# Retention of a streaming encoder: scores of diagonal blocks and running state sums in place of all causal blocks

## The chip, the cores and the metric

The kernel runs on one core of one Trainium2 chip. The time is that of one launch on the device, in microseconds (us). TensorE is the matrix engine (PE in the rows; PEld is its weight load, the load of the stationary operand), VectorE is DVE, ScalarE is ACT, GpSimd is POOL, and SyncE (SP) only issues transfers. The time before is 2163.48 us, the median of three runs (2162.94 to 2163.66).

## What is computed

Two layers of an encoder, for 512 new tokens of one stream (the prompt) and 32 tokens of a running stream (the sample). A layer is a mixer (a retention branch of 4 heads and an attention branch of 8 heads, merged by gates) and a gated feed-forward. Only the retention changes. In the reference it goes by chunks of 64 tokens, with a state S per head (128 x 256):

```python
scores = einsum('bihd,bjhd->bhij', q, k) * decay            # decay[i,j] = g^(i-j) for i >= j, else 0
o = einsum('bhij,bjhe->bihe', scores, v) + einsum('bihd,bhde->bihe', q, S) * xi
S_new = S * g_len + einsum('bjhd,bjhe->bhde', k * zeta, v)
```

Here g is a number per head just below 1, q and k have 128 columns per head and v has 256. Behind it o is normed per head and token, multiplied by a gate silu(g_r), and projected. The last S is an output. The result does not depend on the length of a chunk, so a kernel may choose another.

## The kernel before, in words

All products that need fp32 precision are made of three matmuls: each operand is split into a high part, rounded to the fp32r type, and a low part, which is the operand less its high part; the three are high x high, high x low and low x high. ScalarE makes the high part (a copy that rounds), VectorE the low part (a subtraction that writes fp32r). For the weights GpSimd does the subtraction.

Each engine has its own program, written out in the order in which it runs: `sync_program`, `pool_program`, `pe_program`, `act_program`, `dve_program`. They meet only at semaphores. `S.up(name, key)` counts one up, and `S.at(name, key)` is the wait for it. `S.own()` is the wait for the engine's own last result. A bank of PSUM is taken by `acquire(bank, act=, dve=)` on TensorE, which waits until ScalarE and VectorE have counted up `act_free_<bank>` and `dve_free_<bank>` for the bank's last user. There are eight banks: mm0 and mm1, used in turn by the projections, s0, s0b, s1, s1b, t and o.

A layer has six phases: S, D (four times, attention), R (retention), M (merge), F and G (feed-forward). The weights come in units of 2048 columns per partition, which are split in two halves of 1024: ScalarE's `hi` (L1157) makes the high half, GpSimd's `lo` (L519) subtracts it from the raw one. ScalarE starts the pair of the next unit ahead of tile 0 of the unit at hand.

Phase R runs over the four heads, and there are two layers, so that the head's part is run 8 times. Per head there are three units of weights: query and key (`rk`), value (`vr`) and gate (`gr`). A unit is multiplied by `n_tile(j, m)` in five tiles of tokens: tile 4 is the 32 samples (fp32 matmuls, L682), and tiles 0 to 3 are 24 matmuls of 256 columns each (L703 to L705). The retention itself stands between the tiles of the gate's unit. TensorE's order for a head, from line 913:

- tiles of the value's unit, then 10 transposes of rotated queries and keys (L726, from `rk`) to banks s0 and s1, as soon as VectorE's rotation is done (key `rope`, L1976 to L1988)
- `n_tile(j, 4)`, `n_tile(j, 0)`, `rscores(0)`, `rscores(1)`, `n_tile(j, 1)`, `rscores(2)`, `rscores(3)`, `n_tile(j, 2)`, `outs(0)`, `outs(1)`, the sample's scores (L981), `n_tile(j, 3)`, `outs(2)`, `outs(3)`, the new state (12 matmuls, L991), the sample's output (L997, L998) and the sample's new state (L1002)

`rscores(jb)` (L936) multiplies the keys of block jb with the queries of blocks jb to 3: 512, 384, 256 and 128 columns, three matmuls each. `outs(ib)` (L950) adds up, for the queries of block ib, the products of the weighted scores with the values of blocks 0 to ib, three matmuls of 256 columns for each pair of blocks.

VectorE's order for a head (L1976 to L2095): the rotation; the low parts of the value's tiles (`value_lo`, L1969), which free the banks mm0 and mm1; the keys times zeta (L1992, key `kz`); the sample's sum (L1760, L1764); `qx` (L1999); the low parts of the transposed queries and keys (L2003); the sample's gate sum (L2045, L2048, key `gsum`), which frees the bank of `n_tile(j, 4)`, the one that `n_tile(j, 1)` takes; then `gate(0)` to `gate(3)` (L2011) with the scores times decay (`decayed`, L2028), their low parts (`decayed_lo`, L2018), and `gated(ib)` (L2038), which multiplies an output block in bank t or o by its gate. ScalarE's `squares(hh, ib)` (L1655) reads the same bank, and both must be through before the bank is taken again. The low part of the keys times zeta (L2069, `kz_lo`) comes late, behind `gated(1)`.

Of the kernel before, what the change touches and what calls it, by code (L numbers as in the profile page):

```python
# [43 lines left out]
F32 = mybir.dt.float32  # L44
F32R = mybir.dt.float32r
# [37 lines left out]
def shape_tables():  # L83
# [16 lines left out]
    rel = np.arange(SEQ, dtype=f)[None, :] - np.arange(P, dtype=f)[:, None]  # L100
    decay = np.where(rel[:, None, :] >= 0, np.exp(log_g[None, :, None] * np.maximum(rel, 0)[:, None, :]), 0) * ks
    zeta = np.zeros((P, TILES, RET_HEADS), f)
    for m in range(NT):
        zeta[:, m] = np.exp(log_g * (SEQ - 1.0 - pos[:, m:m + 1])) * ks
    zeta[:DEC, NT] = np.exp(log_g * (DEC - 1.0 - np.arange(DEC, dtype=f)[:, None])) * ks
    xi = np.exp(log_g[:, None] * (np.arange(DEC, dtype=f) + 1.0))
# [3 lines left out]
        zeta.reshape(P, -1), np.broadcast_to(xi.reshape(1, -1), (P, RET_HEADS * DEC)),  # L110
        np.broadcast_to(np.exp(log_g * f(DEC))[None], (P, RET_HEADS)),
        np.broadcast_to(np.array([[lam[0], lam[1], 1 - lam[0], 1 - lam[1]]]), (P, 4))], axis=1)
    return small.astype(f), np.ascontiguousarray(decay.astype(f).reshape(P, RET_HEADS * SEQ))
# [110 lines left out]
def program(nc, A, known):  # L224
# [4 lines left out]
    with ctx:  # L229
# [29 lines left out]
        nsmall = P + 2 * TILES * 64 + 2 * TILES * 8 + TILES * 4 + 4 * DEC + 4 + 4  # L259
# [13 lines left out]
        zeta = take(TILES * 4).rearrange("p (m h) -> p m h", m=TILES)  # L273
        xi = take(4 * DEC).rearrange("p (h i) -> p h i", h=4)
# [29 lines left out]
        sT_hi = sb("sT_hi", [P, NT * UC], F32R, base)  # L304
        rk_sample = sb("rk_sample", [P, UC], F32, base)
# [18 lines left out]
        with ExitStack() as s:  # L324
            with ExitStack() as s2:
                sT_raw = sb("sT_raw", [P, 1280], F32, s2)
                kz_raw = sb("kz_raw", [P, TILES, RET_DK], F32, s2)
            sT = sb("sT", [P, 1280], F32R, s)
            kz = sb("kz", [P, TILES, RET_DK], F32R, s)
            vrh = sb("vrh", [P, 2, NT, UC], F32R, s)  # L330
            sT_hi2 = sb("sT_hi2", [P, 2 * P], F32R, s)
# [3 lines left out]
            decay = sb("decay", [P, SEQ], F32, s)  # L335
            oret = sb("oret", [P, KC, TILES, P], F32, s)
# [80 lines left out]
        def sync_program(S):  # L417
# [28 lines left out]
            for l in S.layers():  # L446
                for phase, _ in ORDER:
                    for i in S.bodies(phase):
# [25 lines left out]
                        elif phase == "R":  # L474
                            for j, what in enumerate(us):
# [10 lines left out]
                                if j % 3 == 1 and j < 11:  # L486
                                    h = j // 3
                                    e.wait_ge(*(S.at("dve_free_s1", ("snew", h - 1)) if h else S.at("dve_free_s1", k=0)))
                                    e.dma_start(decay[:, :], A["tab_decay"][:, h * SEQ:(h + 1) * SEQ]).then_inc(*S.up("decay_in", ("d", h), n=16))
# [110 lines left out]
        def pe_program(S):  # L600
# [134 lines left out]
            for _ in S.layers():  # L735
# [180 lines left out]
                for _ in S.bodies("R"):  # L916
                    start()
                    tile[0] = 0
                    for hh in range(RET_HEADS):
# [16 lines left out]
                        def rscores(jb):  # L936
                            n = SEQ - jb * P
                            if jb == 0:
                                e.wait_ge(*S.at("act_free_s1", ("qk", hh, 1)))
                                e.wait_ge(*S.at("dve_free_s1", ("qk", hh, 1)))  # L940
                                acquire("s0", dve=2)
                            if jb == 2:
                                acquire("s1", dve=2)
                            bank = "s0" if jb < 2 else "s1"
                            for i, (a, b) in enumerate(((0, 0), (1, 0), (0, 1))):
                                ins = e.matmul(pv(bank, P, n, (jb % 2) * 512), key_part(b)[:, jb * P:(jb + 1) * P], qrT[:, a, jb * P:SEQ],
                                               start=(i == 0), stop=(i == 2))
                            ins.then_inc(*S.up("s_ready", ("ret", hh, jb)))

                        def outs(ib):  # L950
                            bank = "to"[ib % 2]
                            acquire(bank, act=1, dve=1)
                            e.wait_ge(*S.at("dve_step", ("sT_lo", hh, ib)))
                            if hh == 0 and ib == 1:
                                e.wait_ge(*S.at("osum_done", "osum"))
                            if ib == 0:
                                e.wait_ge(*S.at("dve_free_mm0", ("vr", hh, 2)))
                                e.wait_ge(*S.at("dve_free_mm1", ("vr", hh, 3)))
                            for jb in range(ib + 1):
                                o = SOFF[jb] + (ib - jb) * P  # L960
                                hi = sT_hi_part(jb)[:, (ib - jb) * P:(ib - jb + 1) * P]
                                for i, (s, v) in enumerate(((hi, 0), (hi, 1), (sT[:, o:o + P], 0))):
                                    ins = e.matmul(pv(bank, P, RET_DV), s, vrh[:, v, jb, :],  # L963
                                                   start=(jb == 0 and i == 0), stop=(jb == ib and i == 2))
# [5 lines left out]
                        rscores(0)  # L970
                        rscores(1)
# [1445 lines left out]
```

## Time and profile before

| | |
|---|---|
| median of three runs | 2163.48 us |
| the profiled execution's own time | 2163.2 us |
| its span in the trace | 2161.4 us |
| TensorE matmul busy | 2142.2 us, 17696 matmuls |
| VectorE, ScalarE, GpSimd busy | 1207.6, 974.3, 871.0 us |
| granted TensorE clock | 1.00 |
| one head of phase R | 47.25 us, 8 times |

Busy time of TensorE counts every moment at which a matmul is in flight. Matmuls overlap, so the duration of one (283 ns for 256 columns) is not what it costs: that is read from the start of one to the start of the next. A row of a timeline with x2 merges two instructions, and its first number is the start of the first.

### The profile page before, as it was taken

Reading aid. Unit: us, or ns where it says so; the run is one execution under the profiler, and the core shown is the slowest. Engines: PE = TensorE matmul, PEld = TensorE weight load, DVE = VectorE, ACT = ScalarE, POOL = GpSimd, SP = SyncE. Lnnn points to the kernel's source line nnn. Section 1 sums busy time; section 2 is a strip of 40 time slices with the busy share of each in tenths; the row PEclk is TensorE's granted clock in tenths of the full one; section 3 lists DMA queues with packets and bytes.
Section 4 is the critical chain, followed back from the end, with each engine's and each line's share of the span. In section 5 each row is a group of like instructions: output and inputs, shape, how many; then the busy total and the mean of one; then the engine's idle time right before and its main releaser. Section 6 shows DMA issues by size and latency. Waiting matters only on the chain.

```text
span 2161.4 us, 43436 instructions
## 1 busy us (share of the span) xinstructions
PE 2142.2 (99%) x17696; PEld 2080.4 (96%) x17696; DVE 1207.6 (56%) x2107; ACT 974.3 (45%) x1882; POOL 871.0 (40%) x386
## 2 busy tenths in 40 slices
PE   7999999999999999999999999999999999999999
PEld 7899989999999999999998899999999999999999
DVE  6676666556355662266267576655563556623551
ACT  5655564445323452344246655644542335423441
POOL 4344423234433433433463354323343444334433
PEclk9999999999999999999999999999999999999999
DMA  5323222222222222221323233222222222222223
GB/s 176 100 85 114 74 84 86 72 96 79 79 88 89 82 83 82 98 98 61 107 92 101 75 105 100 72 72 89 79 82 95 79 86 92 80 88 98 90 69 109
DMA packets 76405, 193.71 MB, mean 90 GB/s; under 512 B 7760, under 2 KB 28848, under 8 KB 76208
## 3 DMA queue, kind: packets, MB, share of 16 engines
q1 hardware_dynamic: 67712, 184.51, 25.9%
q10 hardware_dynamic: 8496, 6.44, 0.9%
q8 instruction: 141, 2.31, 0.4%
q14 instruction: 56, 0.46, 0.1%
HBM read 177.50 MB, written 13.42 MB: 88 GB/s over the span
## 4 chain that ended last, share of the span: by engine, by line
PE 89%; DVE 7%; ACT 3%; issue 1%; DMA 0%; DVEq 0%; ACTq 0%
PE ps L654 13%; PE ps L656 13%; PE ps L655 13%; PE ps L703 7%; PE ps L704 7%; PE ps L705 7%; PE ps L1093 4%; PE ps L1092 4%; PE ps L1094 4%; DVE nmax L1895 2%; PE ps L682 2%; PE ps L726 2%; PE ps L800 1%; PE ps L802 1%; PE ps L801 1%; PE ps L963 1%
## 5 line engine op out<-in xcount | busy, mean ns | idle before, releaser
L519 POOL TENSOR_TENSOR wlo<-raw,whi 128x1024 fp32r<-128x1024 f32 (+1 forms) x328 | 769.8, 2367 | 1043.0 <-ACT whi L1157 1043.0
L654 PE MATMUL ps<-hl,whi 128*128 128x272 f32 x2432 | 703.0, 289 | 0.0
L656 PE MATMUL ps<-hl,wlo 128*128 128x272 f32 x2432 | 701.0, 288 | 0.0
L655 PE MATMUL ps<-hl,whi 128*128 128x272 f32 x2432 | 699.8, 288 | 0.0
L654 PEld LDWEIGHTS ps<-hl,whi 128*128 128x128 f32 x2432 | 458.7, 189 | 0.0
L656 PEld LDWEIGHTS ps<-hl,wlo 128*128 128x128 f32 x2432 | 457.5, 188 | 0.0
L655 PEld LDWEIGHTS ps<-hl,whi 128*128 128x128 f32 x2432 | 457.1, 188 | 0.0
L1157 ACT ACTIVATE whi<-raw 128x1024 fp32r<-128x1024 f32 (+1 forms) x330 | 314.2, 997 | 204.1 <-PE ps L1094 179.4
L703 PE MATMUL ps<-whi,hl 128*128 128x256 f32 x1216 | 347.0, 285 | 0.0
L704 PE MATMUL ps<-wlo,hl 128*128 128x256 f32 x1216 | 343.0, 282 | 0.0
L705 PE MATMUL ps<-whi,hl 128*128 128x256 f32 x1216 | 342.6, 282 | 0.0
L703 PEld LDWEIGHTS ps<-whi,hl 128*128 128x128 f32 x1216 | 230.1, 189 | 10.7 <-issue 10.7
L705 PEld LDWEIGHTS ps<-whi,hl 128*128 128x128 f32 x1216 | 230.0, 189 | 0.0
L704 PEld LDWEIGHTS ps<-wlo,hl 128*128 128x128 f32 x1216 | 229.4, 189 | 0.0
L1093 PE MATMUL ps<-act,whi 128*128 128x272 f32 (+1 forms) x704 | 203.8, 290 | 0.0
L1092 PE MATMUL ps<-act,whi 128*128 128x272 f32 (+1 forms) x704 | 203.1, 289 | 0.0
L1094 PE MATMUL ps<-act,wlo 128*128 128x272 f32 (+1 forms) x704 | 202.8, 288 | 0.0
L2234 DVE SCALAR_TENSOR_TENSOR ca<-up,par,ca 128x546 f32<-128x546 f32 x176 | 141.6, 804 | 37.2 <-ACT ca L1568 29.5
L1092 PEld LDWEIGHTS ps<-act,whi 128*128 128x128 f32 x704 | 132.9, 189 | 0.3
L1094 PEld LDWEIGHTS ps<-act,wlo 128*128 128x128 f32 x704 | 133.0, 189 | 0.0
L1093 PEld LDWEIGHTS ps<-act,whi 128*128 128x128 f32 x704 | 132.8, 189 | 0.0
L525 POOL TENSOR_TENSOR rstd<-ms,mhalf 128x20 f32<-128x20 f32 x20 | 79.5, 3973 | 109.8 <-DVE ms L1672 108.9
(241 smaller groups left out, 3314.9 us busy)
## 6 DMA issues: line engine op xcount, KB each, us to landing
raw<-in_w_units_dram SPq DMA_DIRECT2D x260, 512.0 KB, 4.7
raw<-in_w_down_units_dram SPq DMA_DIRECT2D x64, 352.0 KB, 3.5
kcT<-in_cache_k_dram SPq DMA_DIRECT2D x16, 256.0 KB, 2.9
out_new_k_prompt_dram<-rawk SPq DMA_DIRECT2D x8, 512.0 KB, 3.0
out_new_v_prompt_dram<-vd SPq DMA_DIRECT2D x8, 512.0 KB, 3.6
raw<-in_w_first_dram SPq DMA_DIRECT2D x6, 512.0 KB, 4.9
vc_n<-in_cache_v_dram SPq DMA_DIRECT2D x8, 256.0 KB, 4.5
vc_n<-in_cache_v_dram ACTq DMA_DIRECT2D x8, 256.0 KB, 2.8
```

Of the source, the lines that this page charges most:

```text
L519: e.tensor_tensor(wlo[:, s, a:b], raw[:, s, a:b], whi[:, s, a:b].bitcast(F32), ALU.subtract).then_inc(*S.up("w_ready", ("lo", j, part)))
L654: e.matmul(out, wh, hi, start=(c == 0), stop=False)
L655: e.matmul(out, wh, lo, start=False, stop=False)
L656: ins = e.matmul(out, wl, hi, start=False, stop=(c == KC - 1))
L703: e.matmul(out, hi, wh, start=(c == 0), stop=False)
L704: e.matmul(out, hi, wl, start=False, stop=False)
L705: ins = e.matmul(out, lo, wh, start=False, stop=(c == KC - 1))
L1092: e.matmul(out, wh, hi, start=(k == 0), stop=False)
L1093: e.matmul(out, wh, lo, start=False, stop=False)
L1094: ins = e.matmul(out, wl, hi, start=False, stop=(k == FB - 1))
L1157: e.activation(whi[:, s, a:b], raw[:, s, a:b], ACT.Copy).then_inc(*S.up("hi_ready", ("hi", j, part)))
L2234: e.scalar_tensor_tensor(out=ca[:, s, :], in0=up[:, j % 2, s, v:v + GP], scalar=w(2 + v, j, s), in1=ca[:, s, :], op0=ALU.mult, op1=ALU.add ...
```

## The change

Queries and keys are scaled ahead of the transposes: the query of token t by g^(t-511), its key by g^(511-t) (the table `zeta` has both now). Their product then has the decay g^(i-j) by itself, and the scores need only a mask of zeros and ones (`causal`), the same for every head. So scores are formed for the four diagonal blocks alone (`block_scores`). The blocks on their left are reached through sums: `state(m)` is the product of the scaled keys and the values of block m, `part_sum(m)` adds it to a running sum, and `outs(ib)` multiplies the query block with the sum of the blocks before it (`past`). The last sum is the new state, so that the 12 matmuls of L991 are the same ones, in four pieces. The table of decays and its transfers go.

```diff
-        sT_hi = sb("sT_hi", [P, NT * UC], F32R, base)
+        sb("rk_space", [P, TILES, UC], F32, base)
...
+            zq = sb("zq", [P, TILES, 2, RET_DK], F32, s)
+            sT_raw = sb("sT_raw", [P, NT, P], F32, s)
+            sT = sb("sT", [P, 2, NT, P], F32R, s)
+            kz = sb("kz", [P, NT, RET_DK], F32R, s)
+            past = sb("past", [P, 2, NT - 1, RET_DV], F32R, s)
+            state_sum = sb("state_sum", [P, RET_DV], F32, s)
...
-                                    e.dma_start(decay[:, :], A["tab_decay"][:, h * SEQ:(h + 1) * SEQ])...
```

TensorE:

```diff
-                        e.wait_ge(*S.at("dve_step", ("rope", hh)))
+                        e.wait_ge(*S.at("dve_step", ("zq", hh)))
                         for v in range(2):
-                            feature_transposes(lambda m: rk[:, m, v * P:(v + 1) * P], f"s{v}", ("qk", hh, v), 1, 1)
+                            feature_transposes(lambda m: zq[:, m, v, :], f"s{v}", ("qk", hh, v), 1, 1)
...
+                        def block_scores():
+                            e.wait_ge(*S.at("act_free_s1", ("qk", hh, 1)))
+                            e.wait_ge(*S.at("dve_free_s1", ("qk", hh, 1)))
+                            acquire("s0", dve=2)
+                            for b in range(NT):
+                                tokens = slice(b * P, (b + 1) * P)
+                                for i, (q, k) in enumerate(((0, 0), (1, 0), (0, 1))):
+                                    ins = e.matmul(pv("s0", P, P, b * P), key_part(k)[:, tokens], qrT[:, q, tokens], start=(i == 0), stop=(i == 2))
+                            ins.then_inc(*S.up("s_ready", ("ret", hh)))
+                            for i, (q, k) in enumerate(((0, 0), (1, 0), (0, 1))):
+                                ins = e.matmul(pv("s0b", P, DEC), key_part(k)[:, SEQ:SEQ + P], qrT[:, q, SEQ:TOK], start=(i == 0), stop=(i == 2))
+                            ins.then_inc(*S.up("s_ready", ("rets", hh)))
+                        def state(m):
+                            bank = PART_BANKS[m % 2]
+                            acquire(bank, dve=1)
+                            if m == 0:
+                                e.wait_ge(*S.at("dve_free_mm0", ("vr", hh, 2)))
+                                e.wait_ge(*S.at("dve_free_mm1", ("vr", hh, 3)))
+                                e.wait_ge(*S.at("dve_step", ("kz_lo", hh)))
+                            for i, (z, v) in enumerate(((kzh, 0), (kzh, 1), (kz, 0))):
+                                ins = e.matmul(pv(bank, P, RET_DV), z[:, m, :], vrh[:, v, m, :], start=(i == 0), stop=(i == 2))
...
                         def outs(ib):
-                            for jb in range(ib + 1):
-                                o = SOFF[jb] + (ib - jb) * P
-                                hi = sT_hi_part(jb)[:, (ib - jb) * P:(ib - jb + 1) * P]
-                                for i, (s, v) in enumerate(((hi, 0), (hi, 1), (sT[:, o:o + P], 0))):
+                            for i, (a, v) in enumerate(((0, 0), (0, 1), (1, 0))):
+                                ins = e.matmul(pv(bank, P, RET_DV), sT[:, a, ib, :], vrh[:, v, ib, :], start=(i == 0), stop=(ib == 0 and i == 2))
+                            if ib:
+                                e.wait_ge(*S.at("dve_step", ("past_lo", hh, ib - 1)))
+                                for i, (a, v) in enumerate(((0, 0), (0, 1), (1, 0))):
+                                    ins = e.matmul(pv(bank, P, RET_DV), qrT[:, a, ib * P:(ib + 1) * P], past[:, v, ib - 1, :], start=False, stop=(i == 2))
...
-                        rscores(0)
-                        rscores(1)
+                        block_scores()
+                        state(0)
                         n_tile(j, 1, hl1, dve=1, act=1)
-                        rscores(2)
-                        rscores(3)
+                        state(1)
+                        outs(0)
                         n_tile(j, 2, hl1, dve=1, act=1)
-                        outs(0)
+                        state(2)
                         outs(1)
...
                         n_tile(j, 3, hl1, dve=1, act=1)
+                        state(3)
                         outs(2)
                         outs(3)
...
+                        acquire("s0", dve=1)
+                        e.matmul(pv("s0", P, RET_DV), zq[:, NT, 1, :], rk[:, NT, :], start=True, stop=True)...
                         acquire("t", act=1, dve=1)
```

VectorE and ScalarE:

```diff
+                        e.tensor_tensor(zq[:, :, :, :], rk[:, :, :].rearrange("p m (v d) -> p m v d", v=2),
+                                        zeta[:, :, :, head:head + 1].broadcast_to([P, TILES, 2, P]), ALU.mult)...
                         value_lo(2)
-                        e.tensor_tensor(kz_raw[:, :, :], rk[:, :, P:2 * P], zeta[...], ALU.mult)...
                         value_lo(3)
...
+                        e.wait_ge(*S.at("act_step", ("kzh", hh)))
+                        e.wait_ge(*S.own())
+                        e.tensor_tensor(kz[:, :, :], zq[:, 0:NT, 1, :], kzh[:, :, :].bitcast(F32), ALU.subtract)...
...
                         gate(0)
-                        decayed(0)
-                        decayed(1)
-                        decayed_lo(0)
-                        decayed_lo(1)
+                        masked()
+                        part_sum(0)
+                        masked_lo()
+                        part_lo(0)
                         gate(1)
...
                         gate(3)
+                        part_sum(3)
                         gated(2)
                         gated(3)
...
                                 if u == 2 and m in (2, 3):
-                                    for ib in ((0, 1) if m == 2 else (2, 3)):
-                                        squares(S, e, hh, ib)
+                                    squares(S, e, hh, m - 2)
...
+                        squares(S, e, hh, 2)
+                        squares(S, e, hh, 3)
                         squares(S, e, hh, NT)
```

`masked` is the scores times the mask, for the four blocks and for the sample; `masked_lo` their low part (a subtraction of 512 columns, SBUF to SBUF); `part_lo(m)` the low part of a running sum. ScalarE copies the high parts behind the tanh of gate tiles 0, 1 and 2. SyncE loses its transfer of the decays.

VectorE's order in the second head of a layer, from the end of the rotation to the first gate, before (`kz_raw` are the keys times zeta, `vrh` the value's tiles, `rest` the sample's sums):

```order
L1988 TENSOR_TENSOR rawq<-rawq,kz_raw 128x10x64
L1969 SCALAR_TENSOR_TENSOR vrh<-ps,rs,vrh 128x256
L1992 TENSOR_TENSOR kz_raw<-rawq,small 128x640
L1969 SCALAR_TENSOR_TENSOR vrh<-ps,rs,vrh 128x256
L1760 SCALAR_TENSOR_TENSOR rest<-ps,rs,rest 32x256 x2
L1764 SCALAR_TENSOR_TENSOR rawq<-ps,rs,rest 32x256
L1999 TENSOR_TENSOR qx<-ps,small 128x32
L2003 TENSOR_TENSOR qrT<-ps,qrT 128x544
L2003 TENSOR_TENSOR krT_lo<-ps,krT 128x640
L2045 TENSOR_TENSOR rest<-ps,rest 32x256 x2
L2048 TENSOR_TENSOR rest<-ps,rest 32x256
L2011 SCALAR_TENSOR_TENSOR oret<-oret,ps 128x2x128
```

and the same stretch of the changed kernel:

```order
L1974 TENSOR_TENSOR rawq<-rawq,zq 128x10x64
L1977 TENSOR_TENSOR zq<-rawq,small 128x1280
L1955 SCALAR_TENSOR_TENSOR vrh<-ps,rs,vrh 128x256 x2
L1746 SCALAR_TENSOR_TENSOR rest<-ps,rs,rest 32x256 x2
L1750 SCALAR_TENSOR_TENSOR rawq<-ps,rs,rest 32x256
L1986 TENSOR_SCALAR qx<-ps,small 128x32
L1990 TENSOR_TENSOR qrT<-ps,qrT 128x544
L1990 TENSOR_TENSOR krT_lo<-ps,krT 128x640
L1994 TENSOR_TENSOR kz<-zq,kzh 128x512
L2057 TENSOR_TENSOR rest<-ps,rest 32x256 x2
L2060 TENSOR_TENSOR rest<-ps,rest 32x256
L2002 SCALAR_TENSOR_TENSOR oret<-oret,ps 128x2x128
```

The scaling has grown from 640 to 1280 columns and stands ahead of the value's low parts, where the transposes wait for it; the low part of the scaled keys now stands ahead of the sample's sums.

TensorE's order in the same head of the changed kernel, from the last two blocks of scores to the first matmul of gate tile 1 (`kzh` and `kz` are the parts of the scaled keys):

```order
L941 MATMUL ps<-qrT,krT 128x128 x2
L941 MATMUL ps<-qrT,krT_lo 128x128
L944 MATMUL ps<-qrT,krT 128x32 x2
L944 MATMUL ps<-qrT,krT_lo 128x32
L956 MATMUL ps<-vrh,kzh 128x256 x2
L956 MATMUL ps<-vrh,kz 128x256
L700 MATMUL ps<-whi,hl 128x256
```

Before, six matmuls of L946 (512 and 384 columns) stood ahead of that tile, and the three of 32 columns (L981) two tiles later.

## Rows read from the trace of the kernel before

**Rows 1.** The page's first part: busy time and share of the span.
```profile
PE 2142.2 (99%) x17696; PEld 2080.4 (96%) x17696; DVE 1207.6 (56%) x2107; ACT 974.3 (45%) x1882; POOL 871.0 (40%) x386
```
**Rows 2.** Waits of PE, whole span: us in total, times, longest us.
```profile
PE ps L746 <- DVE wlo L1709: 12.0, 1, 12.0
```
**Rows 3.** Timeline of PE, first head: start us, us, engine, line, operation.
```profile
324.53 0.62 PE L946 MATMUL ps<-qrT,krT 128*128 128x512 f32 x2
...
325.74 0.28 PE L703 MATMUL ps<-whi,hl 128*128 128x256 f32 x1
...
328.95 0.33 PE L946 MATMUL ps<-qrT,krT 128*128 128x128 f32 x2
...
329.23 0.33 PE L703 MATMUL ps<-whi,hl 128*128 128x256 f32 x1
329.40 0.28 PE L704 MATMUL ps<-wlo,hl 128*128 128x256 f32 x1
...
332.14 0.40 PE L963 MATMUL ps<-vrh,sT_hi 128*128 128x256 f32 x2
...
332.49 0.40 PE L963 MATMUL ps<-vrh,sT_hi 128*128 128x256 f32 x2
```
**Rows 4.** Timeline of DVE, second head, from the rotation to the scores' low parts.
```profile
360.30 1.16 DVE L1983 TENSOR_TENSOR rawq<-rawq,small 128x640 f32<-128x640 f32 x1
...
364.44 0.83 DVE L1988 TENSOR_TENSOR rawq<-rawq,kz_raw 128x640 f32<-128x640 f32 x1
...
370.27 0.81 DVE L2003 TENSOR_TENSOR krT_lo<-ps,krT 128x640 fp32r<-128x640 f32 x1
371.19 0.88 DVE L2045 TENSOR_TENSOR rest<-ps,rest 32x256 f32<-32x256 f32 x2
372.10 0.41 DVE L2048 TENSOR_TENSOR rest<-ps,rest 32x256 f32<-32x256 f32 x1
...
374.63 2.37 DVE L2018 TENSOR_TENSOR sT<-sT_raw,sT_hi 128x512 fp32r<-128x512 f32 x2
```
**Rows 5.** Timeline of POOL, second head.
```profile
358.38 5.34 POOL L519 TENSOR_TENSOR wlo<-raw,whi 128x1024 fp32r<-128x1024 f32 x2 [7.07 <-ACT whi L1157]
371.02 4.77 POOL L519 TENSOR_TENSOR wlo<-raw,whi 128x1024 fp32r<-128x1024 f32 x2 [7.30 <-ACT whi L1157]
```
**Rows 6.** Instructions of line 2069, eight heads: duration ns min/median/max.
```profile
L2069 DVE TENSOR_TENSOR kz<-kz_raw,kzh x8: 692/693/694, 334.7 to 1548.7; 128x512 fp32r<-128x512 f32 x8
```
**Rows 7.** Timeline of PE, second head: the first scores.
```profile
371.75 0.62 PE L946 MATMUL ps<-qrT,krT 128*128 128x512 f32 x2
```
**Rows 8.** Timeline of PEld (weight loads), second head.
```profile
366.49 1.12 PEld L726 LDWEIGHTS ps<-small,rawq 128*128 128x128 f32 x10
...
383.53 0.31 PEld L963 LDWEIGHTS ps<-vrh,sT_hi 128*128 128x128 f32 x2
...
387.83 0.40 PEld L998 LDWEIGHTS ps<-sq,qx 128*128 128x128 f32 x2
388.26 0.41 PEld L1002 LDWEIGHTS ps<-rawq,kz_raw 128*128 128x128 f32 x2
```
**Rows 9.** Timeline of DVE, then ACT, second head: outs(2) is gated and squared.
```profile
384.92 0.42 DVE L2038 TENSOR_TENSOR oret<-ps,oret 128x256 f32<-128x256 f32 x1
...
385.38 0.39 ACT L1662 ACTIVATE sq<-ps 128x256 f32<-128x256 f32 x1 [1.06 <-DVE oret L2038]
385.66 0.20 ACT L1662 ACTIVATION_READ_ACCUMULATOR sq<-ps 128x1 f32 x1
```
**Rows 10.** Timelines of DVE and PEld in phase D: a result, and who waits.
```profile
136.54 0.35 DVE L1917 SCALAR_TENSOR_TENSOR prob<-prob,rinv 128x128 f32<-128x128 f32 x1
...
137.10 0.14 PEld L857 LDWEIGHTS ps<-small,prob 128*128 128x128 f32 x1
```
**Rows 11.** Timelines of DVE and PEld, first head: rotation's end, transposes.
```profile
316.81 0.82 DVE L1988 TENSOR_TENSOR rawq<-rawq,kz_raw 128x640 f32<-128x640 f32 x1
...
319.27 1.12 PEld L726 LDWEIGHTS ps<-small,rawq 128*128 128x128 f32 x10
```

More of the change, by code:

```diff
@@ L999, in pe_program @@
                             *S.up("t_ready", ("os", hh)))
-                        acquire("s1", dve=1)
-                        e.matmul(pv("s1", P, RET_DV), kz_raw[:, NT, :], rk[:, NT, :], start=True, stop=True).then_inc(
-                            *S.up("s_ready", ("snew", hh)))
                 for _ in S.bodies("M"):
@@ L1998, in dve_program @@
                         e.wait_ge(*S.own())
-                        e.tensor_tensor(qx[:, 0:DEC], pv("s0", P, DEC, SEQ), xi[:, head, :], ALU.mult).then_inc(
+                        e.tensor_scalar(qx[:, 0:DEC], pv("s0", P, DEC, SEQ), g32[:, head:head + 1], None, ALU.mult).then_inc(
                             *S.up("dve_step", key=("qx0", hh)))
@@ new lines, in masked, with masked_lo @@
+                            e.wait_ge(*S.at("s_ready", ("rets", hh)))
+                            e.wait_ge(*S.own())
+                            e.tensor_tensor(sTs_x[0:DEC, 0:DEC], pv("s0b", DEC, DEC), causal[0:DEC, 0:DEC], ALU.mult).then_inc(
+                                *S.up("dve_free_s0", ("sTs", hh)))
+                        def masked_lo():
+                            e.wait_ge(*S.at("act_step", ("sT", hh)))
+                            e.wait_ge(*S.own())
+                            e.tensor_tensor(sT[:, 1, :, :], sT_raw[:, :, :], sT[:, 0, :, :].bitcast(F32), ALU.subtract).then_inc(
+                                *S.up("dve_step", key=("sT_lo", hh)))
@@ new lines, in part_sum @@
+                        def part_sum(m):
+                            bank = PART_BANKS[m % 2]
+                            e.wait_ge(*S.at("s_ready", ("part", hh, m)))
+                            if m == NT - 1:
+                                e.wait_ge(*(S.at("st_out0", ("st", hh - 1)) if hh else S.at("st_out0", k=0)))
+                            e.wait_ge(*S.own())
+                            if m == 0:
+                                ins = e.tensor_copy(state_sum[:, :], pv(bank, P, RET_DV))
+                            else:
+                                ins = e.tensor_tensor(sout[:, 0, :] if m == NT - 1 else state_sum[:, :], pv(bank, P, RET_DV), state_sum[:, :], ALU.add)
+                            ins.then_inc(*S.up(f"dve_free_{bank}", ("part", hh, m)))
@@ L2031, in gated, with part_lo @@
+                        def part_lo(m):
+                            e.wait_ge(*S.at("act_step", ("past", hh, m)))
+                            e.wait_ge(*S.own())
+                            e.tensor_tensor(past[:, 1, m, :], state_sum[:, :], past[:, 0, m, :].bitcast(F32), ALU.subtract).then_inc(
+                                *S.up("dve_step", key=("past_lo", hh, m)))
                         def gated(ib):
```

153 lines of the change are left out of this document (47 added, 106 removed).

## The prediction, made before the changed kernel was run

> **What bounds the kernel now.** I read the page's busy times first: a matmul is in flight for 99% of the span [rows 1]. Then the waits of TensorE: the longest entry is a single one of 12.0 us while the first weights are made ready [rows 2], and none of its entries lies in the retention. So TensorE's instruction stream is the time, and in phase R it has no holes. Whatever is taken out of it is gained in full, and whatever makes it wait is lost in full. Every other engine matters only where it hands something to TensorE, so the second reading is of margins: the timelines of VectorE, GpSimd and ScalarE in one head. The head runs 8 times, and its pattern repeats to within 0.2 us.
>
> **What TensorE loses in work.** Costs are distances from start to start. `rscores(0)` and `rscores(1)` take 324.53 to 325.74 = 1.21 us. The last three matmuls of 128 columns take 328.95 to 329.23 = 0.28, and the matmul behind them comes 0.17 after the next instead of the usual 0.12, so 0.33 in all: 0.11 for each [rows 3]. Three of 256 columns take 0.35 (332.14 to 332.49) [rows 3], 0.12 each. The old scores so cost 1.21 + 0.35 + 0.33 = 1.89 us per head. The new ones are 12 matmuls of 128 columns at 0.11 = 1.32: half the columns and more are gone, but a narrow matmul costs nearly what one of 256 does, because each brings a weight load of its own. Saved: 0.57. The outputs go from 30 matmuls to 21 (12 on the diagonal, 9 with the sums), 9 x 0.12 = 1.08 saved. The state's 12, the sample's matmuls and the transposes stay in number. Together **1.65 us saved per head**, 13.2 in all. The Trainium skill, "TensorE: Matmul & The Clock Gate", section "Wait — 56ns, not 53.3ns?", gives N / 2.4 GHz + about 2.5 ns from start to start, 56 ns for 128 columns. By that rule the new scores would be 0.67 and the old ones 1.63, and the forecast some 2.5 us lower; the rows' 0.11 speaks against it here, where every matmul loads new weights, and the sum goes by the rows.
>
> **First wait: the transposes.** They waited for the end of the rotation, and now wait for a multiplication of 1280 columns behind it. No row has that size. 256 columns take 0.41 and 640 take 0.83 [rows 4], which is 0.42 for 384 more; the next 640 add 0.70, and 1280 take 1.5. The bounds are 0.83 (its half) and 1.66 (twice that). From a result of VectorE to the weight load that waits for it go 0.21 us (136.54 + 0.35 to 137.10) [rows 10]. In the second head the rotation ends at 364.44 + 0.83 = 365.27 [rows 4]; the multiplication then ends at about 366.8, and the weight load may start at 367.0. It started at 366.49 [rows 8]. So 0.5 us of wait (0 to 0.7). In the first head of a layer it is 316.81 + 0.82 = 317.63, plus 1.5 and 0.21, 319.35, against 319.27 [rows 11]: 0.1. `value_lo(2)` and `value_lo(3)` are moved behind it, but their banks are wanted only after 10 transposes, which is more than their 0.48 each: nothing. The separate multiplication of 640 columns that goes is not on the path.
>
> **Second wait: the low part of the scaled keys**, and this one decides. It moves ahead of the sample's gate sum. It is a subtraction of 512 columns from SBUF to SBUF that took 0.69 us in all eight heads, late in the head with GpSimd idle [rows 6]. Where GpSimd's subtraction of weights runs, the like do not take that. In the trace of before, two low parts of scores (512 and 384 columns) issued at 374.63 took 2.37 where 0.69 + 0.56 would do [rows 4]: the extra 1.1 us is what GpSimd had left of its pair, which ends at 371.02 + 4.77 = 375.79 [rows 5]. The rotation's product at 360.30 took 1.16 instead of 0.83: it got in when the first half ended (358.38 + 2.39 = 360.77), and GpSimd's pair grew from 4.77 to 5.34 [rows 4, 5]. So each instruction holds the other out for its whole length, and VectorE gets in between two halves. Instructions that read a bank of PSUM are not held: the sample's gate sum at 371.19 ran its 0.88 right under GpSimd's [rows 4, 5]. The moved subtraction takes just the place of that sum: issued at 371.19, while GpSimd has begun at 371.02. It waits to 371.02 + 2.39 = 373.41 and ends at 374.10. The gate sum follows 0.11 later (the gap from `krT_lo` to it, 371.08 to 371.19) and takes 372.10 + 0.41 - 371.19 = 1.32 [rows 4], to 375.53. TensorE wants that bank for `n_tile(j, 1)`: 371.75 [rows 7] plus 15 narrow matmuls at 0.11 and the three of `state(0)` at 0.12 gives 373.76. It gets it at 375.53 + 0.21, and the first matmul comes 0.12 later, 375.86. **2.1 us of wait**. `state(0)` waits for the same subtraction, inside the same hole. The bounds are 0 (the subtraction goes first: gate sum at 373.2 + 0.21, in time) and 4.5 (it waits for both halves).
>
> Behind it all else is shifted alike. The masked scores (0.69 like the other 512 columns), ScalarE's copy, the copy of the sum and `masked_lo` (0.69) need about 2.9 us from the gate sum on, and TensorE has a tile of 24 matmuls and `state(1)`, 3.2 us; GpSimd's second half, pushed to 374.1, is over at 376.5, before `masked_lo` is issued. Nothing, then, though the cover is thin. `past_lo(0)` to `past_lo(2)` have most of a tile each.
>
> **Third wait: the end of the head.** The state's four products stood between `outs(3)` and the sample's output, which takes bank t again; three of them now lie before the last tile, and one ahead of `outs(2)`. TensorE's first weight load behind tile 3 is at 383.53; 15 matmuls at 0.12 (`state(3)`, two outputs of six) and the sample's state (387.83 to 388.26, 0.43) bring it to 385.76 [rows 8]. Bank t is free when `gated(2)` and its square are done. `gated(2)` ran at 384.92; `part_sum(3)` goes ahead of it now (0.42 and a gap of 0.11), so 385.45 to 385.87; the square and the read of its sum end 0.48 after they start (385.38 to 385.86) [rows 9], 386.39, and TensorE hears of it at most 0.2 later: 386.5. **0.7 us of wait** (0.3 to 1.0). Part of it falls at bank o, whose `squares(1)` is now behind the tanh of tile 3.
>
> ScalarE has fewer columns to copy, and SyncE one transfer fewer per head; the wait for `snew` ahead of SyncE's load of the state is the same event under another bank's name. None is on the path.
>
> **The sum.** Six heads: -1.65 + 0.5 + 2.1 + 0.7 = +1.65, 9.9 us. Two first heads: -1.65 + 0.1 + 2.1 + 0.7 = +1.25, 2.5 us. The profiled execution took 2163.2 us, so 2175.6; the median of the runs lies 0.3 above it, **2175.9 us**, slower by 0.6%. Its own range, by the bounds of the three waits, is 2169 to 2182.
>
> **The rivals.**
> *VectorE gets in first.* The two requests are 0.17 us apart [rows 4, 5]; if `qx`, now another form of instruction, or a copy of ScalarE's shifts that, the subtraction ends at 371.9, GpSimd's pair runs to 376.7, and the gate sum is in time. But then `masked_lo`, issued near 375.5, is held to 376.7, ends at 377.4, and `outs(0)` waits some 0.7. With the other waits a head comes to +0.25 (first heads -0.15): about 2165. For it: the distance is small. Against it: GpSimd was ahead in all eight heads. Chance 0.14.
> *Faster: neither subtraction is held.* If VectorE and GpSimd work side by side on these operands, the second wait is gone and a head comes to -0.45 (first heads -0.85): 2159. If the multiplication of 1280 columns and the end of the head fit in their margins too, it is the whole 13.2 us, 2150. The point is whether the gate sum ends before 373.4. Against it: rows of the same form, stretched in every head. Chance 0.13.
> *Held through both halves.* If GpSimd's second half goes first, 2.4 us more per head, 2195. The rotation's product got in between, eight times. Chance 0.05.
> *The scores are not cheaper.* If a narrow matmul into a bank shared by four blocks costs twice the 0.11, 1.3 us more per head, 2186; three in a row show nothing of it. Chance 0.03.
> The rest, 0.65, is the forecast.
>
> **How the numbers follow.** A measurement of this kernel tells about 0.2% from no change, 4.3 us: faster is below 2159.2, slower above 2167.8. Slower: the forecast less a little at its lower edge, the third and the fourth rival, 0.70. Same: the first rival and a share of the second's 2159, 0.17. Faster: 0.13. The range reaches from 2159, to take in the first rival and the edge of the second, to 2182, the upper end of the forecast's own; about 2 in 10 is left out.
>
> **What would show it.** Right: in every head the new low part of the keys with 2.5 to 3 us instead of 0.69, GpSimd's pair grown by 0.7 just there, a hole of about 2 us ahead of the first matmul of gate tile 1, smaller ones at the transposes and ahead of the sample's output, and 72 fewer matmuls. Wrong: the subtraction at 0.69 with GpSimd's first half starting behind it, narrow scores apart by other than 0.11, or a head shorter than the old one.

## The result, and the profile after

The changed kernel takes 2180.32 us (median of 5 runs, 2179.89 to 2181.86) against 2162.94 us for the one before (5 runs, 2162.16 to 2163.66): 17.4 us slower, a ratio of 1.0081 with a 95% interval of 1.0068 to 1.0094. The forecast was 2175.9 in a range of 2159 to 2182, and slower with a chance of 0.70. The direction and the mechanism held, and the time lies in the range, near its upper end; the loss of 17.4 us is 5 us more than the 12.4 that the sum gave.

The changed kernel's page, first the span and the busy times [rows 1]:

```profile
span 2178.5 us, 43278 instructions
PE 2142.9 (98%) x17624; PEld 2073.0 (95%) x17624; DVE 1230.4 (56%) x2115; ACT 970.1 (45%) x1874; POOL 872.1 (40%) x386
```

There are 72 matmuls fewer, and the span is 17.1 us longer. TensorE has less to do and takes longer over it: it waits. Its waits are where one reads on [rows 2]. This is the view of waits of the changed kernel, for PE (us in total, times, longest us) and then for PEld, where a wait shows as the idle time ahead of a weight load:

```profile
PE ps L743 <- DVE wlo L1695: 11.9, 1, 11.9
PE ps L700 <- DVE rest L2060: 7.1, 8, 1.2
PE ps L956 <- DVE kz L1994: 4.6, 8, 0.6
PE ps L672 <- DVE sq L2090: 2.7, 2, 1.3
```
```profile
PEld ps L700 <- issue: 19.4, 35, 1.4
PEld ps L956 <- issue: 5.1, 8, 0.7
PEld ps L996 <- ACT sq L1648: 3.8, 8, 0.5
PEld ps L672 <- issue: 3.4, 2, 1.7
PEld ps L967 <- ACT sq L1648: 2.1, 8, 0.3
PEld ps L723 <- DVE zq L1977: 2.0, 7, 0.3
```

Each of the eight heads now has a wait for the low part of the scaled keys (L956) and one for the gate sum's bank (L700), the two halves of one hole; two at the end of the head, at bank o (L967) and at bank t (L996); seven have one at the transposes (L723). L672 was in no list of mine: it is a fourth wait, twice, at the start of phase M.

The hole, in the second head. First VectorE, then GpSimd, then the weight loads of TensorE, three timelines [rows 4, 5, 8]:

```profile
371.17 0.81 DVE L1990 TENSOR_TENSOR krT_lo<-ps,krT 128x640 fp32r<-128x640 f32 x1
372.09 2.69 DVE L1994 TENSOR_TENSOR kz<-zq,kzh 128x512 fp32r<-128x512 f32 x1
374.89 0.88 DVE L2057 TENSOR_TENSOR rest<-ps,rest 32x256 f32<-32x256 f32 x2
375.80 0.41 DVE L2060 TENSOR_TENSOR rest<-ps,rest 32x256 f32<-32x256 f32 x1
```
```profile
371.86 5.15 POOL L516 TENSOR_TENSOR wlo<-raw,whi 128x1024 fp32r<-128x1024 f32 x2 [7.57 <-ACT whi L1148]
```
```profile
374.06 0.19 PEld L944 LDWEIGHTS ps<-qrT,krT_lo 128*128 128x128 f32 x1
374.90 0.30 PEld L956 LDWEIGHTS ps<-vrh,kzh 128*128 128x128 f32 x2 [0.65 <-issue]
375.13 0.19 PEld L956 LDWEIGHTS ps<-vrh,kz 128*128 128x128 f32 x1
376.33 0.19 PEld L700 LDWEIGHTS ps<-whi,hl 128*128 128x128 f32 x1 [1.01 <-issue]
```

The subtraction of 512 columns was issued at 372.09, 0.23 us behind GpSimd's start, and took 2.69 us in place of 0.69 [rows 6]. The gate sum, which reads PSUM, ran at its usual 0.88 and 0.41, but from 374.89 on. TensorE's weight loads stood for 0.65 and then for 1.01 us.

One more thing is in this trace. Its windows, two heads of the first layer and two of the second, then 4 us of the second head (us; busy us and instructions of PE, PEld, DVE, ACT, POOL; granted clock; DMA):

```profile
367.40:417.20 49.80, 48.19 (x400) 45.07 (x400) 30.25 (x48) 21.49 (x45) 16.37 (x7) 0.97 0.23 73
417.20:465.50 48.30, 46.67 (x400) 43.55 (x400) 30.30 (x48) 21.51 (x45) 16.38 (x7) 1.00 0.23 74
1399.10:1448.80 49.70, 48.15 (x400) 45.03 (x400) 30.17 (x48) 21.44 (x45) 16.36 (x7) 0.97 0.22 73
1448.80:1497.10 48.30, 46.67 (x400) 43.54 (x400) 30.30 (x48) 21.52 (x45) 16.38 (x7) 1.00 0.23 75
```
```profile
376.00:378.00 2.00, 1.64 (x11) 1.67 (x12) 1.58 (x5) 0.43 (x1) 1.00 (x1) 0.79 0.00 0
378.00:380.00 2.00, 2.00 (x11) 2.00 (x11) 1.47 (x3) 0.62 (x2) 0.00 (x0) 0.50 0.00 0
380.00:382.00 2.00, 2.00 (x17) 2.00 (x17) 0.42 (x1) 0.47 (x1) 0.00 (x0) 0.86 0.00 0
```

The heads have two lengths, 48.3 and 49.8 us, where before all had 47.2. The 400 matmuls are the same. In the longer ones the granted clock falls to 0.50, the 1.2 GHz level, for 3.4 us behind the hole (TensorE had stood for most of 374.3 to 376.3), and 11 matmuls pass in 2 us instead of 19. That happened in three of the eight heads of this execution, 1.5 us each, 4.5 us together. Not every hole does this. The fourth wait leaves one of 1.7 us at the start of phase M in each layer, and there the clock stays at 1.00:

```profile
490.09 0.52 PEld L672 LDWEIGHTS ps<-small,rs 128*128 128x128 f32 x5 [1.71 <-issue]
```
```profile
488.00:494.00 6.00, 4.67 (x36) 4.27 (x35) 2.21 (x7) 3.02 (x10) 1.17 (x1) 1.00 0.14 46
```

The first row is that hole in the first layer, the second the stretch around it. By the Trainium skill, "TensorE: Matmul & The Clock Gate", section "What's actually happening", the throttled state is the default and activity releases it; the trace agrees in so far as each of the three falls stands behind a hole; which holes bring one these rows do not tell.

**Where the 17.1 us come from.** The rows of idle weight loads name the waits: transposes 2.0, hole 5.1 + 8.7 (L700's 19.4 less the 10.7 that it had before the change), end of the head 3.8 + 2.1, phase M 3.4. For a sum they are too short. A weight load lasts 0.19 us, but in a stream without waits the next one begins 0.11 or 0.12 after it, so that a wait costs some 0.07 more than the idle time in its row. In the second head 2.27 us pass from the load at 374.06 to the one at 376.33, where without waits it would be 0.11 + 3 x 0.12 = 0.47: 1.80 us lost, and the rows show 0.65 + 1.01.

Distances have no such gap. From the first transpose of one head to that of the next it is 47.22 us before and 48.29 now, if the clock stays at 1.00: 1.07 more, net of the work saved. Six such distances make 6.4 us, and three falls of the clock 4.5. The other 6.2 us lie behind the last head of each layer (2.6 and 3.1, with phase M's wait of 1.7 in each) and ahead of the second layer's first head (0.65), less 0.17 at the start.

### The profile page after: what moved, and what is told of

Its sections match the earlier page's. It is cut to its first block, busy times and chain, and to the rows that moved or that the text cites. A ratio compares the mean times of both kernels' runs of the same rounds, so it can differ in the third digit from the quotient of the medians.

```text
span 2178.5 us, 43278 instructions
## 1 busy us (share of the span) xinstructions
PE 2142.9 (98%) x17624; PEld 2073.0 (95%) x17624; DVE 1230.4 (56%) x2115; ACT 970.1 (45%) x1874; POOL 872.1 (40%) x386
## 4 chain that ended last, share of the span: by engine, by line
PE 82%; DVE 12%; ACT 3%; issue 1%; DMA 0%; DVEq 0%; POOL 0%; ACTq 0%
PE ps L651 13%; PE ps L653 13%; PE ps L652 13%; PE ps L700 6%; PE ps L701 6%; PE ps L702 6%; PE ps L1088 4%; PE ps L1087 4%; PE ps L1089 4%; DVE nmax L1881 2%; PE ps L723 2%; PE ps L797 1%; PE ps L799 1%; PE ps L798 1%; PE ps L679 1%
## 5 line engine op out<-in xcount | busy, mean ns | idle before, releaser
L700 PE MATMUL ps<-whi,hl 128*128 128x256 f32 x1216 | 348.9, 287 | 7.6 <-DVE rest L2060 7.1
L700 PEld LDWEIGHTS ps<-whi,hl 128*128 128x128 f32 x1216 | 232.3, 191 | 20.3 <-issue 19.4
```

The costliest lines, as they stand in the source:

```text
L700: e.matmul(out, hi, wh, start=(c == 0), stop=False)
```

## The experiments

Two theories of the hole. *Theory 1*: GpSimd's weight subtraction holds VectorE's out for its whole length. *Theory 2*: the subtraction is slow by itself, by its operands or by its place behind ScalarE's copy, or nothing is held and only the queue got longer. The first four runs test these and the fourth wait.

**GpSimd waits for the low part of the keys.** In the changed kernel's GpSimd program:

```diff
                     for j in range(1, UNITS["R"] + 1):
+                        if j % 3 == 2:
+                            e.wait_ge(*S.at("dve_step", ("kz_lo", j // 3)))
                         lo("R", j)
```

> The changed kernel, but GpSimd waits with its weight subtraction for the low part of the scaled keys, so that VectorE's subtraction is never issued into a running one of GpSimd. Theory 1 (GpSimd holds it out): it takes 0.69 us instead of 2.69, the hole ahead of gate tile 1 (about 2 us per head) is gone, and with it the three stretches of 3.4 us at a granted clock of 0.50; but masked_lo is now issued into GpSimd's second half, takes some 1.9 us, and outs(0) waits about 0.7 us per head. 2180.3 - 8 x 2.1 - 4.5 + 8 x 0.75 = 2165. Theory 2 (the subtraction is slow by its own operands or its place behind ScalarE's copy, and GpSimd is beside the point): it stays at 2.7 us, and so does the hole: 2180, or more by what the weights come late.

Measured: 2165.66 us (11 runs, 2165.01 to 2166.66), 1.0014 of before (1.0005 to 1.0022). VectorE and GpSimd of this run, second head:

```profile
370.42 0.69 DVE L1996 TENSOR_TENSOR kz<-zq,kzh 128x512 fp32r<-128x512 f32 x1
371.21 0.88 DVE L2059 TENSOR_TENSOR rest<-ps,rest 32x256 f32<-32x256 f32 x2
...
374.78 1.70 DVE L2022 TENSOR_TENSOR sT<-sT_raw,sT 128x512 fp32r<-128x512 f32 x1
```
```profile
371.19 4.75 POOL L516 TENSOR_TENSOR wlo<-raw,whi 128x1024 fp32r<-128x1024 f32 x2 [8.57 <-DVE kz L1996]
```

The same instruction with the same operands in the same place takes 0.69 us once GpSimd is not running. Theory 2 is out. The cost has gone to the next subtraction from SBUF to SBUF: `masked_lo` took 1.70, and `outs(0)` waited for it (weight loads of L969 idle 3.6 us in eight heads, against none). That is the mechanism of my first rival, only that it had to be forced. Its price, 2165, fits by some luck: this run has the 3.4 us of phase M, which the rival's sum had not, and a wait at `outs(0)` below the 0.7 us per head that it had. The clock stayed at 1.00 throughout.

**Gate sum first.** On VectorE alone:

```diff
-                        e.tensor_tensor(kz[:, :, :], zq[:, 0:NT, 1, :], kzh[:, :, :].bitcast(F32), ALU.subtract)...
...
                             *S.up(f"dve_free_{bank}", ("gsum", hh)))
+                        e.tensor_tensor(kz[:, :, :], zq[:, 0:NT, 1, :], kzh[:, :, :].bitcast(F32), ALU.subtract)...
                         gate(0)
```

> The changed kernel, with the low part of the scaled keys moved behind the sample's gate sum on VectorE; TensorE's order stays. Theory 1: it is issued at 1.4 us later into the same GpSimd instruction and ends at the same moment, 2.7 us after GpSimd's start, so state(0) waits as before (0.6 to 0.7 us per head), but the bank of gate tile 1 is free in time: the hole shrinks from 2.0 to about 0.7 us, no stretch at clock 0.50: 2180.3 - 8 x 1.3 - 4.5 = 2165. Theory 2: the subtraction takes 2.7 us from its later start, state(0) waits 1.4 us longer than now and the hole keeps its length: 2180.

Measured: 2167.11 us (11 runs, 2166.6 to 2167.93), 1.0021 (1.0012 to 1.003). Its VectorE and GpSimd, second head:

```profile
370.70 0.88 DVE L2053 TENSOR_TENSOR rest<-ps,rest 32x256 f32<-32x256 f32 x2
371.62 0.41 DVE L2056 TENSOR_TENSOR rest<-ps,rest 32x256 f32<-32x256 f32 x1
372.13 1.27 DVE L2060 TENSOR_TENSOR kz<-zq,kzh 128x512 fp32r<-128x512 f32 x1
```
```profile
370.48 5.18 POOL L516 TENSOR_TENSOR wlo<-raw,whi 128x1024 fp32r<-128x1024 f32 x2 [7.57 <-ACT whi L1148]
```

Issued 1.6 us behind GpSimd's start it took 1.27, issued 0.23 behind it 2.69: in both cases it ends 2.9 us after that start (2.92 in each). So its duration says only how much of GpSimd's half was left. `state(0)` waits as before (5.1 us in eight heads), the bank is free in time (L700 back to 11.0 us), and the clock does not fall, behind these eight short holes or behind phase M's two of 1.7 and 1.8 us. One line in another place gained 13.2 us.

**And `state(0)` behind gate tile 1**, with its sum behind `gate(1)` and ScalarE's copy of that sum behind the tanh of tile 1 in place of tile 0 (not shown):

```diff
                         block_scores()
-                        state(0)
                         n_tile(j, 1, hl1, dve=1, act=1)
+                        state(0)
                         state(1)
...
                         masked()
-                        part_sum(0)
                         masked_lo()
-                        part_lo(0)
                         gate(1)
+                        part_sum(0)
+                        part_lo(0)
                         part_sum(1)
```

> As the run before, and state(0) moved behind gate tile 1 on TensorE, with its sum behind gate(1) on VectorE. Theory 1: no hole at all ahead of gate tile 1: 2180.3 - 8 x 2.1 - 4.5 = 2159, below the kernel before by some 4 us. If the clock did not fall because of that hole, the stretches at 0.50 stay and it is 2163.5. Theory 2: the subtraction is still 2.7 us, hidden behind the tile; gate(0) comes late, the masked scores with it, and outs(0) waits: 2163 to 2168.

Measured: 2161.51 us (11 runs, 2161.02 to 2162.14), 0.9995 (0.9986 to 1.0004): no difference from before that can be measured. The wait of L956 is gone from the list and nothing stands in its place. It is 2.5 us above what was expected, as the run before was 2.1 above: the hole was 1.80 us per head and not the 2.1 I had put down, 8 x 0.3 us.

**The spread of phase M in other banks.**

```diff
-                    spread("s0", "s0b")
+                    spread("s1", "s1b")
```

> The changed kernel, with the first transposes of phase M (the spread of the norms) in banks s1 and s1b instead of s0 and s0b. The theory of a fourth wait (bank s0 is held by the last head's new state of the sample until VectorE has read it, behind the sample's output): the wait of 1.7 us at the start of phase M goes in both layers: 2180.3 - 3.4 = 2176.9. Its rival (the spread waits for the norms' own values, whichever bank it takes): 2180.3.

Measured: 2175.28 us (5 runs, 2174.97 to 2177.68), 1.0061 (1.0049 to 1.0074): 5.0 us less. The waits of L672 (2.7 us of PE, 3.4 of PEld) are out of its list, the waits of the heads are to the tenth those of the changed kernel. Most of the other 1.6 us is a fall of the clock less, two heads instead of three in its profile. The rival, that the spread waits for the norms' own values, is out. So the bank is the cause: the change gave the sample's new state to s0, VectorE reads it last of all in a head, and the next phase begins with s0.

The other four runs: the same suspicion in the kernel before, the remaining waits, and all of them at once.

**One line of the change in the kernel before**: its low part of the keys (L2069) moved ahead of its gate sum, nothing else.

```diff
+                        e.tensor_tensor(kz[:, 0:NT, :], kz_raw[:, 0:NT, :], kzh[:, :, :].bitcast(F32), ALU.subtract)...
...
                         gated(1)
...
-                        e.tensor_tensor(kz[:, 0:NT, :], kz_raw[:, 0:NT, :], kzh[:, :, :].bitcast(F32), ALU.subtract)...
                         gate(3)
```

> The kernel before, with one thing of the change alone: the low part of the scaled keys moved ahead of the sample's gate sum on VectorE. Theory 1 (held by GpSimd's weight subtraction): it takes 2.7 us there, the gate sum ends near 375.6 instead of 372.5 in the second head, and gate tile 1 waits some 2.9 us per head: 8 x 2.9 = 23 us, and a hole this long should bring TensorE's clock to 0.50 for 3.4 us in some or all heads, 1.5 us each: 2162.7 + 23 + 0 to 13 = 2186 to 2199. Theory 2 (no hold, only 0.69 us more in the queue, of which 0.1 is margin): 8 x 0.6 = 5 us, 2167.5, and no fall of the clock.

Measured: 2196.03 us (4 runs, 2194.07 to 2196.91), 1.0153 (1.014 to 1.0167). VectorE, the weight loads, and a window over one head:

```profile
374.98 2.78 DVE L2007 TENSOR_TENSOR kz<-kz_raw,kzh 128x512 fp32r<-128x512 f32 x1
```
```profile
379.30 0.19 PEld L703 LDWEIGHTS ps<-whi,hl 128*128 128x128 f32 x1 [2.70 <-issue]
```
```profile
382.00:434.00 52.00, 49.59 (x413) 47.05 (x412) 29.72 (x47) 21.88 (x45) 16.38 (x7) 0.96 0.22 74
```

An instruction of 0.69 us, moved, costs 33 us. Per head it is 2.7 us of hole, and the clock fell in all eight, not in three; the heads are 51.3 to 51.4 us apart instead of 47.2. Behind a hole of 2.7 us it fell each time. Behind the pair of 0.65 and 1.01 it fell in some heads only: 3, 2, 4 and 2 of eight, in the four profiled executions that have the pair (changed kernel, spread in s1, old order, scaling in halves); in two heads of the one with the old order the fall began inside the second hole of the pair, 0.4 to 0.5 us ahead of its end. Behind the single 0.65 of the run with the gate sum first it never fell, nor behind phase M's 1.7 us, twice in each of six profiled executions. So the length of one hole does not settle it, and no run shows what does.

**The end of a head in the old order.**

```diff
                         n_tile(j, 3, hl1, dve=1, act=1)
-                        state(3)
                         outs(2)
                         outs(3)
+                        state(3)
...
                         gate(3)
-                        part_sum(3)
                         gated(2)
                         gated(3)
+                        part_sum(3)
...
-                                if u == 2 and m in (2, 3):
-                                    squares(S, e, hh, m - 2)
+                                if u == 2 and m == 2:
+                                    squares(S, e, hh, 0)
+                                    squares(S, e, hh, 1)
```

> The changed kernel with the end of a head in the old order: state(3) behind outs(3), its sum on VectorE behind the two gated outputs, squares of outputs 0 and 1 both behind the tanh of tile 2. The theory of the third wait (0.3 us at bank o and 0.5 at bank t per head): both go, 8 x 0.75 = 6 us: 2174. If the end of a head is bound by the output's own chain and not by this order, nothing changes: 2180.

Measured: 2175.16 us (5 runs, 2173.35 to 2177.16), 1.0056 (1.0042 to 1.007). The wait at bank o is gone, the one at bank t is 2.0 us instead of 3.8: 3.9 of 5.9 us, so not both in full. Its row of waits:

```profile
PEld ps L996 <- ACT sq L1649: 2.0, 8, 0.2
```

The profiled execution, with four falls of the clock, is the slowest of the five (2177.16, mean granted clock 0.997; the fastest, 2173.35, has 0.999, the other three 0.998): the hole is still there, and how often the clock falls behind it goes with the 3.8 us over which these runs spread.

**The scaling in two halves.**

```diff
-                        e.tensor_tensor(zq[:, :, :, :], rk[...], zeta[...].broadcast_to([P, TILES, 2, P]), ALU.mult)...("zq", hh)
+                        for v in range(2):
+                            e.tensor_tensor(zq[:, :, v, :], rk[:, :, v * P:(v + 1) * P],
+                                            zeta[:, :, v, head:head + 1].broadcast_to([P, TILES, P]), ALU.mult)...(("zq0", "zq")[v], hh)
...
-                        e.wait_ge(*S.at("dve_step", ("zq", hh)))
                         for v in range(2):
+                            e.wait_ge(*S.at("dve_step", (("zq0", "zq")[v], hh)))
```

> The changed kernel with the scaling in two multiplications of 640 columns, queries first, and the transposes of the queries waiting for the first alone. The theory of the first wait (0.3 us in seven heads): the first ends 0.67 us sooner, the transposes do not wait; the second costs a start more on VectorE (0.05 us) and is hidden by five transposes (0.6 us) or nearly: -2 us: 2178. Rival: the transposes of the keys wait in their place, and the low parts of the value's tiles are later: 2180 or slightly more.

Measured: 2177.39 us (5 runs, 2174.86 to 2179.72), 1.0068 (1.0056 to 1.0081): 2.9 us less. The wait of L723 for `zq` is out of the list. Its runs lie 4.9 us apart, and its profile has two falls of the clock where the changed kernel's has three (1.5 us), so the 2.9 by itself would not prove much; the row does, and so does the distance between heads, 0.27 us shorter.

**All of them together**: gate sum first, `state(0)` behind tile 1, the spread in s1, the old order at the end of a head, the scaling in halves.

> All mended together: gate sum ahead of the low part of the keys, state(0) behind gate tile 1, the end of the head in the old order, the scaling in halves, the spread in banks s1 and s1b. If the saved matmuls are worth what their distances say (0.57 + 1.08 = 1.65 us per head) and no wait is left, it is 2162.7 - 13.2 = 2149.5. If a narrow score matmul or one of the sums costs more than read, or another wait comes up in place of these, it stays above 2153.

Measured: 2150.64 us (5 runs, 2150.41 to 2152.14), 0.9946 (0.9933 to 0.9958): 12 us faster than the kernel before, and 30 us faster than the change as it was made, with the same matmuls. Its page and TensorE's waits:

```profile
span 2148.6 us, 43292 instructions
PE 2130.1 (99%) x17624; PEld 2067.3 (96%) x17624; DVE 1216.2 (57%) x2123; ACT 970.7 (45%) x1874; POOL 874.2 (41%) x386
```
```profile
PE ps L743 <- DVE wlo L1696: 11.3, 1, 11.3
PE ps L854 <- DVE prob L1904: 2.0, 8, 0.2
PE ps L723 <- DVE hl L2141: 0.9, 2, 0.4
```

The list is that of the kernel before again, but for one entry of 0.2 us (L871). The transposes of two heads are 45.65 us apart, 1.57 less than before, with 0.2 us of wait at bank t left: the work saved is 1.77 us per head.

The distances between the transposes of two heads add up (medians in us, of heads without a fall of the clock):

| | distance | change |
|---|---|---|
| before | 47.22 | |
| changed kernel | 48.29 | |
| gate sum first | 47.23 | -1.06 |
| and `state(0)` behind gate tile 1 | 46.51 | -0.72 |
| old order at the end of a head | 47.74 | -0.55 |
| scaling in halves | 48.03 | -0.27 |
| all of them | 45.65 | -2.64 |

The change of `state(0)` is against the run before it, the others' against the changed kernel. The four make -2.60 one by one and -2.64 together.

## Why the prediction was right, and where it was off

- **The bound.** TensorE's stream was the time, and what was taken out of it or put into it came through in full: the four parts of the table add up to the last run. That held.
- **The work saved** was put at 1.65 us per head and is 1.77 by the version without the holes. Twelve narrow matmuls went 0.11 us apart in the changed kernel too: from 372.61, the first of the scores, to 373.89, the first behind them, 1.28 us. These two rows of PE in the changed kernel, second head, are the ends:

```profile
372.61 0.34 PE L941 MATMUL ps<-qrT,krT 128*128 128x128 f32 x2
...
373.89 0.34 PE L944 MATMUL ps<-qrT,krT 128*128 128x32 f32 x2
```

  The 56 ns that the Trainium skill gives for 128 columns ("TensorE: Matmul & The Clock Gate", section "Wait — 56ns, not 53.3ns?") is not what this stream shows, in which each matmul has its own fp32r weight load: 0.11 us, and the same with 32 columns. That the weight load is the reason was argued in the prediction, and no run tests it.
- **The first wait** was put at 3.2 us and is 2.0 (idle weight loads, seven heads). The multiplication took 1.49 us, as read off two sizes. What was mis-sized is the 0.21 us from a result to the weight load that waits for it. `zq` was ready at 365.86 + 1.49 = 367.35, and the load began at 367.40; behind `kz` and `rest` it is 0.12. The row that I had taken it from [rows 10] had another load ahead of it in TensorE's queue, so that it was no latency, only a bound from above.
- **The second wait** was put at 2.1 us per head with its mechanism: behind GpSimd's half, at 0.69 more, the gate sum after it. Issue to end was forecast as 2.91 and is 2.69; TensorE loses 1.80 us per head. The other 0.3 are small: the subtraction ended 2.92 behind GpSimd's start and not 3.08, the weight load came 0.12 behind the result and not 0.21, and the matmul 0.03 behind its load (376.36) and not 0.12. GpSimd's pair grew by 0.4 and not by the 0.7 that was to show it: read so, the two do not hold each other out for quite their whole length. The run in which GpSimd waits shows the cause, and the one line moved in the kernel before shows its price alone.
- **The third wait** was put at 5.6 us and is 5.9, in the two parts that the text named.
- **What failed** is the sentence that nothing else lay on the path. "The wait for `snew` ahead of SyncE's load of the state is the same event under another bank's name" looked at one of those who wait for that bank and not at the other: phase M's first transposes. 3.4 us, shown by the run with the spread moved. And the cost of a hole was taken to be its length: TensorE's clock falls behind some of them, 4.5 us in the profiled execution. Both are outside the sum of the prediction. Its three waits and its saving gave +12.4. By the distances they give 1.07 us per head, 0.3 less in the very first, whose transposes do not wait: +8.3, to which 3.4 and 4.5 come, 16.2 of 17.1. Of the rest 0.35 is a longer hole in the last head (1.4 us of idle at L700 where the others have 1.01); half a microsecond stays unassigned. So the sum's own terms were 4 us too high and it lacked 8: that the total came within 5 us is in part luck.
- **The range.** "2169 to 2182, by the bounds of the three waits" used those of the first and the third only, with the second kept at 2.1; its own bounds, 0 and 4.5, went into the rivals. Worked out so, the upper end is 2181.
- **The rivals.** "VectorE gets in first" was real as a mechanism, but did not occur by itself. That neither subtraction is held, or that both halves of GpSimd go first, is excluded by the rows: 0.69 us where GpSimd waits, and an end 2.92 us after GpSimd's start in the changed kernel and in the one with the gate sum first. That the narrow scores cost twice their price is excluded by the 1.28 us above. GpSimd's pair grew from 4.77 to 5.15, which fits VectorE getting in between the halves. By the Trainium skill, "SBUF — State Buffer", section "SBUF: two separate sides", whichever of the two starts first has the shared port pair for the whole instruction; the rows agree on who waits for whom, and within 0.2 to 0.3 us on the length (2.92 for 3.08, 0.4 for 0.7).

## What to carry to other kernels

Where one engine's stream is the time, a saving in it is worth what its margins leave: list, for each step that is moved ahead, what now waits behind it and when that was wanted, bank by bank and through to the next phase. A subtraction from SBUF to SBUF on VectorE has no fixed price beside a busy GpSimd; put it where the other is idle, or where a tile of matmuls covers the whole of GpSimd's instruction. Here the change as designed was a gain of 12 us, and the order in which it was written turned it into a loss of 17.

## What was not expected of the hardware

- A hole in TensorE's stream can cost more than itself: the granted clock went to 0.50 for 3.4 us, 1.5 us of time, in 3 of 8 heads behind holes of 0.65 and 1.01 us with three matmuls between, and in 8 of 8 behind 2.7 us. It did not do so behind single holes of 0.65 us, nor behind the single one of 1.7 us at the start of phase M, in any profiled execution. What decides it is open.
- A matmul of 32 or 128 columns with its own weight load follows the one before at 0.11 us, one of 256 columns at 0.12: cutting scores from 1280 to 512 columns per head in the same 12 matmuls brought only about a third of their time.
